# A decoder step with gathered experts: other places for the dot products, one U row fewer, a second Z

## What is computed

```python
x = rms_norm(x); q_lat, c_kv, k_pe, rq, rk, rv, rg = split(x @ w_in)      # mixer_inputs
mla = causal_attention(queries(q_lat), keys_values(c_kv, k_pe))           # 8 heads
ret, R_new = retention(rq, rk, rv, R0, chunk=128)                         # 8 heads, with state
h = x + concat([mla, silu(rg) * head_group_norm(ret)]) @ w_o
# PEER: product-key experts, 8 heads x top 16 of 16384 for every token
s1, s2 = q[:, :, 0] @ sub_keys1, q[:, :, 1] @ sub_keys2                   # q = rms_norm(h) @ w_peer_q
vs, experts = top16(top16(s1) + top16(s2)); g = softmax(vs)
act = gelu(einsum('nd,nhkd->nhk', xb, peer_u[experts]))
y = h + einsum('nhk,nhkd->nd', g * act, peer_v[experts])
```

## Time and profile before

| | us |
|---|---|
| median of 3 runs | 3891.19 (3883.03 to 3903.62) |
| the profiled execution | 3887.91 |
| its span | 3886.1 |

### The profile page before, as it was taken

How to read it: one execution, slowest core, us unless ns; L and a number is a source line. 1 busy time by engine, 2 the same in 40 slices (tenths; PEclk the granted TensorE clock), 3 DMA queues, 4 the chain that set the end, 5 groups by cost and what they waited for, 6 DMA issues and landing times.

```text
span 3886.1 us, 35398 instructions
## 1 busy us (share of the span) xinstructions
PE 2539.2 (65%) x11810; PEld 1306.0 (34%) x11810; DVE 2376.2 (61%) x6243; ACT 410.6 (11%) x951; POOL 2360.6 (61%) x2118
## 2 busy tenths in 40 slices
PE   6656656677656677666676766667656776567466
PEld 5642223333334334442233322342334333315001
DVE  3666366676566666766567664756565764857541
ACT  1101000012100121001100110001000110000000
POOL 0146636565755666656766676567765776576775
PEclk8777868788788877788787887888777888775678
DMA  4587959997999889999999999999999999999898
GB/s 172 218 322 306 403 203 409 356 344 298 343 386 364 325 297 358 384 362 375 365 406 373 387 359 379 377 380 384 375 411 350 393 374 376 361 387 365 331 364 333
DMA packets 376057, 1365.51 MB, mean 351 GB/s; under 512 B 61122, under 2 KB 72578, under 8 KB 348354
## 3 DMA queue, kind: packets, MB, share of 16 engines
q0 software_dynamic: 304128, 1107.43, 74.7%
q1 hardware_dynamic: 71746, 255.81, 17.1%
HBM read 1356.76 MB, written 6.31 MB: 351 GB/s over the span
## 4 chain that ended last, share of the span: by engine, by line
PE 20%; POOL 19%; DMA 16%; issue 15%; DVE 15%; another core or an unknown queue 12%; SPq 1%; ACT 1%; DVEq 0%; POOLq 0%; ACTq 0%
POOL v_ring L670 10%; POOL u_ring L659 9%; DMA v_ring<-down_rows,codesT 8%; PE ps L740 6%; DMA wbuf<-weights 6%; PE ps L714 5%; DVE u_ring L1439 3%; DVE arena L1409 3%; DMA u_ring<-up_rows,codes 2%; PE ps L901 2%; PE ps L952 2%; DVE idx L1409 1%; DVE top_c L1409 1%; DVE top_v L1409 1%
## 5 line engine op out<-in xcount | busy, mean ns | idle before, releaser
L670 POOL DMA_INDIRECT v_ring<-down_rows,codesT x1056 | 1173.2, 1111 | 790.7 <-PE ps L714 400.2
L659 POOL DMA_INDIRECT u_ring<-up_rows,codes x1056 | 1186.1, 1123 | 722.1 <-issue 304.8
L1439 DVE CUSTOM_DVE_ANT_0 u_ring<-u_ring,xn 128x1024 f32<-128x1024 f32 x1056 | 1256.0, 1220 | 602.1 <-DMA u_ring<-up_rows,codes 529.5
L714 PE MATMUL ps<-v_ring,Z 128*32 128x512 f32 x4096 | 1101.0, 790 | 751.3 <-DMA v_ring<-down_rows,codesT 431.7
L714 PEld LDWEIGHTS ps<-v_ring,Z 128*32 128x32 f32 x4096 | 186.5, 127 | 1423.5 <-DMA v_ring<-down_rows,codesT 736.1
L740 PE MATMUL ps<-wbuf,xT 128*128 128x256 f32 (+1 forms) x2016 | 515.5, 419 | 198.1 <-DMA wbuf<-weights 174.6
L740 PEld LDWEIGHTS ps<-wbuf,xT 128*128 128x128 f32 (+1 forms) x2016 | 399.2, 205 | 338.4 <-DMA wbuf<-weights 152.5
L901 PE MATMUL ps<-xT,wbuf 128*128 128x128 f32 (+1 forms) x2304 | 331.4, 304 | 54.6 <-DMA wbuf<-weights 33.1
L901 PEld LDWEIGHTS ps<-xT,wbuf 128*128 128x128 f32 x2304 | 310.5, 217 | 141.3 <-issue 98.6
L1409 DVE MAX8 vals<-arena 128x8 f32<-128x128 f32 (+1 forms) x288 | 69.1, 280 | 130.5 <-ACT arena L1264 103.3
L858 PE MATMUL ps<-kT,qT 96*128 96x512 f32 (+3 forms) x192 | 91.2, 587 | 28.1 <-DVE nb L1413 16.8
(11 more groups left out here) (294 smaller groups left out, 2194.3 us busy)
## 6 DMA issues: line engine op xcount, KB each, us to landing
wbuf<-weights SPq DMA_DIRECT2D x215, 1024.0 KB
u_ring<-up_rows,codes POOLq DMA_INDIRECT x1056
v_ring<-down_rows,codesT POOLq DMA_INDIRECT x1056
resid<-x_prompt SPq DMA_DIRECT2D x8, 512.0 KB
table<-decay_in SPq DMA_DIRECT2D x8, 512.0 KB
table<-ffn_w SPq DMA_DIRECT2D x8, 512.0 KB
kT<-cache_latent SPq DMA_DIRECT2D x64, 64.0 KB
y_prompt<-arena SPq DMA_DIRECT2D x8, 512.0 KB
```

Of the source, the lines that this page charges most:

```text
L659: pool.indirect_dma_start(out=u_ring[:, i % U_RING, :], out_offset=None, in_=up_rows, in_offset=bass.IndirectOffsetOnAxis(ap=codes[:, t % ...
L670: pool.indirect_dma_start(out=v_ring[:, v % V_RING, :], out_offset=None, in_=down_rows, in_offset=bass.IndirectOffsetOnAxis(ap=codesT[:, t ...
L714: mm = pe.matmul(acc[32 * c:32 * c + 32, half, :], (Zs if t == TILES else Z)[:, at:at + GS], v_ring[:, v % V_RING, half * 512:(half + 1) * ...
L1439: dve.tensor_tensor_reduce(u, u, xn[:, t % 2], 1.0, 0.0, ALU.mult, ALU.add, dots[:, k:k + 1]).then_inc(dot_done, 1)
```

## The change

The U ring gets 7 buffers, and `Z` gets a second half that groups take in turn; a group's `make_Z` then waits on the V rounds of the group before last. A U buffer and a half of `Z` have the same size. The tables get more and smaller numbers, and each engine gets the calls of `slots()` that go with them. In tiles 1 to 3 the slots of the attention go down from 24 (tile 1), 24 and 26 to 12 (tile 1), 12 and 14, and those of the sample's part go up from 37 to 44, from 33 to 44 and from 31 to 42; the projections take one more, OUT one less, and tile 1's to 3's QKV has 12 instead of 11. The sum over a front stays 95.

```diff
-U_RING, V_RING = 8, 9
+U_RING, V_RING = 7, 9
-        Z = sb("Z", [P, GS * GS])
+        Z = sb("Z", [P, 2, GS * GS])
-        QKV = [4, 4, 4, 3]
+        QKV = [3, 2, 3, 3, 2, 2]
-        OUT = [5, 5, 5, 3]
+        OUT = [5, 5, 3, 3, 2]
-        FRONTS[1] = [2, 2, 3, 2, 3, 3] + [3, 3, 3, 2] + [2] * H + [2, 2] + [5, 5, 5, 5, 5, 4, 4, 4] + [3, 3, 3, 3]
-        FRONTS[2] = [2, 2, 3, 2, 3, 3] + [3, 3, 3, 2] + [2, 2, 2, 3, 2, 2, 3, 2] + [3, 3] + [5, 5, 5, 5, 5, 4, 4] + [3, 3, 3, 3]
+        FRONTS[1] = [3, 2, 3, 2, 3, 3] + [2] * 6 + [1] * H + [2, 2] + [3, 3, 4, 3, 4, 4, 4, 4, 4, 3, 3, 2, 3] + [3, 2, 2, 2, 2]
+        FRONTS[2] = [3, 2, 3, 2, 3, 3] + [2] * 6 + [1, 2, 1, 1, 2, 1, 1, 1, 1, 1] + [3] + [3, 3, 2] * BATCH + [3, 2, 2, 2] + [3, 2, 2, 2, 2]
...
-        LAST = [10, 9, 6, 5] + [4, 0] * H + [0, 0] + [80]
+        LAST = [9, 9, 5, 5, 4] + [3, 3] * H + [2, 2] + [58]
...
-                elif group_no(t, g) >= 1:
-                    act.wait_ge(v_done, group_no(t, g) * GS)
+                elif group_no(t, g) >= 2:
+                    act.wait_ge(v_done, (group_no(t, g) - 1) * GS)
...
-            def qkv(t):
+            def qkv(t, slots):
                 do_signal(kd_ready, t + 1, dve.tensor_tensor, heads(kd), heads(rk[:]), over(dec_k[:], 2, [P, H, 64]), ALU.mult)
+                slots()
                 dve.wait_ge(squares, square_no(t, 3))
...
                 root(P, 16)
+                slots()
                 dve.wait_ge(raw_ready, t + 1)
...
+                    if s == 6 and t == S_TILE:
+                        norm_in(TILES, ST)
                     slots()
...
+                    if j == 5:
+                        slots()
                     dve.wait_ge(kn_sq, m + 1)
```

More of the change, by code:

```diff
@@ L749, in project_all @@
                 for w in range(N_IN):
+                    if t == TILES and w == 4:
+                        pe.wait_ge(wide_ready, wide_no(S_TILE, 1))
                     if 0 < t < TILES and w == 4:
@@ L1006, in sample_batch @@
                         pages_turn(b + 1)
-                    key_norms(b, uk)
+                    slots()
+                    key_norms(b, uk, slots)
                     slots()
@@ L1045, in sample_mixer @@
                     a = 64 * (h % 2)
+                    if h == 5:
+                        slots()
                     if h >= 2:
@@ L1165, in norm_in @@
                         act.wait_ge(y_stored, 16 * (t - 2))
-                own.raises(square_sum(of_s(t, x_s, resid)[0:n, :], n, D, 0), squares, square_no(t, 1))
+                own.raises(square_sum(of_s(t, x_s, resid)[0:n, :], n, D, 0, of_s(t, xn_s, junk)), squares, square_no(t, 1))
             def lat_squares(t, n):
@@ L1365, in sample_batch @@
                         pages_turned(b + 1)
-                    key_squares(b)
+                    slots()
+                    key_squares(b, slots)
                     slots()
@@ L1750, in prompt_front @@
                 project(t, P, slots)
-                qkv(t)
+                qkv(t, slots)
                 slots()
@@ L1815, in sample_retention @@
                 for h in range(H):
+                    if h == 4:
+                        slots()
                     dve.wait_ge(s_cross_ps, h + 1)
@@ L1917, in sample_batch @@
                         pages_keys(b + 1)
-                    key_sums(b)
+                    slots()
+                    key_sums(b, slots)
                     slots()
```

40 lines of the change are left out of this document (27 added, 13 removed).

## The result

The changed kernel takes 3784.9 us (median of 4 runs, 3773.5 to 3789.7) against 3897.4 us for the kernel before (4 runs, 3883.0 to 3926.4): a ratio of 0.9698, with a 95% interval of 0.9637 to 0.9760. That is 3.0% faster, or 103 us between the two profiled executions (3785.0 against 3887.9). The forecast was 3804, so it was 19 us too high, on the right side and inside the stated range of 3755 to 3885.

A forecast was written before the change was run, and what follows sets the result against it. Bytes bound stages with DMA share about 1.0, engine chains the others, leaving 168 us of idle DMA to fill. Terms -81 + 8 - 18 - 4 + 11 + 0 = -84, from 3887.9 to 3804 us; range 3755 to 3885.

The forecast's parts named there:

- A: Attention of tiles 1 to 3: giving up 12 slots each shortens the stages to 38, 41 and 46 us, -81 us.
- B: Sample's part of tiles 1 to 3: taking 7, 11 and 11 more slots costs +8 us in sum.
- The first rival: Sample's stages are the bound and absorb all the gain: some 3880 us, range 3872 to 3900; chance 0.13.
- C: Finer QKV places: half of 36 us idle DMA in tiles 1 to 3, -18 us; nothing in tiles 4 to 7.
- D: Last tile, sample rows' output projection: new places halve POOL's 8.46 us wait for dots, -4 us.
- E: Seven U rows: POOL's 51 waits for a dot each begin one dot earlier, +11 us, ends 0 and +62.
- The rule set against E: U ring: a gather takes 3.2 us, two in flight fill the engines, so seven rows cost 0; sum 3793 us.
- The rival in which the ring turns the sign: Steady part: the smaller U ring holds back V gathers and both rings run dry, 3910 to 3930 us; chance 0.11.
- F: Second half of Z: `make_Z` hardly waits on V rounds, so it brings 0, at best -3 us.

The follow-up runs named there:

- the run of A and B alone: New attention and sample tables of tiles 1 to 3 put into the kernel before, all else old (8 U rows, one Z): ratio 0.9814, 73 us faster.

## Why the prediction was right, point by point

**A**, -81: right in the sum and in what a stage lasts at its end, wrong in where it started. The attention windows give -80, and the stages last 40, 36 and 47 us where 38, 41 and 46 were worked out. But tile 1's stage had 20 slots and 53 us and not 24 slots and 63 us, so it gave -13 and not -25; tiles 2 and 3 gave -34 and -33 and not -29 and -27. That the sum is met to 1 us is luck. Pricing a slot that leaves a stage at full share by its bytes, down to the stage's own chain, was the step that carried the forecast.

**B**, +8: right, +11 by the windows. In the mixer I had +2 and it is -8: the projections, with 21 slots for 29, went from 102 to 76 us (-26, I took -19), and the stretch behind them from 78 to 96 us (+18, I took +21, with every added dot on the chain); in the batches, where I hid most of them and had +3 each, it is +4 and +15. In the batches the four sequences and the softmax behind them take:

```profile
846.00:949.00 103.00, 87.73 (x398) 42.28 (x398) 78.45 (x150) 30.45 (x60) 77.32 (x69) 0.84 0.95 357
949.00:977.00 28.00, 15.42 (x141) 8.47 (x141) 21.75 (x49) 5.68 (x14) 22.51 (x19) 0.70 1.01 396
1293.00:1394.00 101.00, 80.30 (x373) 36.19 (x365) 74.76 (x143) 30.68 (x60) 73.81 (x65) 0.85 0.90 329
```

The sequences were 85 and 84 us, so each became 4 us longer and not 2, which is more than the 90 to 95 us that I had written for all four; the softmax gave back 14 us in tile 2 instead of 5. The two errors cancel in tile 2 and not in tile 3. The first rival, that these stages absorb everything, is refuted by the run of A and B alone.

**C**, -18: the direction was right, the size too small by half or more. The runs give 38 us alone and some 48 to 73 us taken away. Two steps failed. In tiles 1 to 3 I took half of 36 us of idle DMA, and the three QKV windows are shorter by 17, 4 and 8 us of 156 with 12 slots instead of 11, that is 29 us. For tiles 4 to 7 I wrote that nothing is taken, since their share was 0.98 and all their idle time 35 us. The runs showed 20 us less in the changed kernel's trace and 60 us between two kernels on one chip (1748 and 1688), at shares of 0.97 and 0.99. So the distance of the share from 1.00 is not the room that a stage has. Full stages stand at 1.01 to 1.03; measured against these the room was 3 to 5% of 1732 us, an estimated 50 to 85 us and not 35. I had 1.01 in my own windows and took it as 1.

**D**, -4: the wait went, the time didn't come. In the stretch that matches rows 9, 3558 to 3593 us (it is the end of the sample rows' choice of experts, not their output projection: the products with `k1T` and `k2T` stand ahead of it and those with `spread` in it) POOL has no wait for a dot any more, where it had 8.46 us, and the share is 0.96 instead of 0.76. The last tile is no shorter for it; with the old LAST table it lasts 491 us too.

**E**, +11: not decided. Under the new tables the seventh row costs 1 to 3 us with some 15 to either side, under the old ones 21 us (8 to 34); 11 lies in both. In the traces it costs about 10 us in tiles 4 to 7 and 2 to 14 in the last tile. The sum of it uses 0.18, although the 35 of 215 us worked out before it are 16%. Its mechanism is the weak part: it priced POOL's wait for dots alone, and from 8 to 7 rows this wait rose by 139 us while the wait for rounds fell by 86. The rule set against E, by which a gather takes 3.2 us (an estimate from the Trainium skill, DMA: Bandwidth & Descriptors, "Anatomy of one DMA") and the ring would not matter, agrees within the noise with the result at 7 rows and not with that at 6, which cost 34 us. Its "two in flight" doesn't follow from it either: two gathers of 0.52 MB in 3.2 us are an estimated 328 GB/s at most, less than the 383 of rows 2. So a ring of 6 has to cover more than the time of a gather; DVE's stretches without a dot are the likely thing, but no run changed them alone. The rival in which the ring turns the sign had the right place, the steady tiles, as the old tables with 7 rows show, at 21 and 34 us instead of the 115 to 130 that I gave it.

**F**, 0: right. `make_Z` isn't released by a V round in the changed kernel once. With 7 rows and one Z the profile names no V round either; one wait of 10.5 us there has no releaser that it knows.

**The sum.** By the last dots of the stages the 103 us between the two profiled executions are: attention of tiles 1 to 3 -80, the sample's part +11, QKV -29, OUT -8, the choice of experts -3, the projections +18, tiles 4 to 7 -20, the last tile +8. Against the forecast's -84 that is 20 us more in tiles 4 to 7, where I had nothing, 11 more in QKV, 11 for OUT and the choice of experts, and the 11 of the ring, which is no window of its own (what it costs is in the others); and against it 18 us in the projections, 12 in the last tile, 3 in B and 1 in A. So the total is nearer than its parts: about 53 us of gain that I didn't see stand against 34 us of cost that I didn't see, and that they come this near is luck. The projections were a step left out. They take one slot more in each tile, 8 us of bytes, and in tile 1 the stage before (first fence) and after shows a further loss, with a wait of POOL for a dot of 15.52 us that was 7.74 us at most there before:

```profile
217.00:272.00 55.00, 36.49 (x135) 29.47 (x136) 37.80 (x122) 4.06 (x11) 25.20 (x23) 0.81 1.00 361
```

```profile
218.00:283.00 65.00, 42.01 (x161) 34.28 (x162) 38.53 (x122) 4.06 (x11) 27.47 (x23) 0.85 0.94 336
```

```profile
266.12 1.68 POOL L662 DMA_INDIRECT u_ring<-up_rows,codes  x1 [15.52 <-DVE dots L1473]
```

The repeat of the changed kernel needs 59 us for the same stage, so part of this is one execution's. The 8 us of the last tile go with the seventh row and not with the LAST table, by the table of traces above.

## What to carry to other kernels

When one resource is the bound in some stages and idle in others, move work from the first to the second and price it by the bytes that leave, down to the chain that the stage has of its own. Count the slots of a stage from its table before a price is put on them. Price a buffer by what POOL waits for in all, not by its wait for one ring: what a smaller ring adds to the one wait, it takes in part from the other. The longest wait in a trace need not be the price of a buffer; compare the stages of the two kernels to see where the time is. And before a stage is called full, compare its share with the highest that any stage shows, not with 1, and take even that as a rough measure.
